# A gated mLSTM/Fourier mixer on one core: the output gate's sigmoid moves to the projection stage, the head gain into the weight rows

## The chip, the cores and the metric

The kernel runs on one core of one Trainium2 chip. The metric is the device time of the whole program in microseconds, as the median of several runs; lower is better. The engines are named as in the profile: PE is TensorE (PEld its weight loads), DVE is VectorE, ACT is ScalarE, POOL is GpSimd, SP is SyncE, which here only issues DMAs.

## The reference, cut to what matters

One layer is applied to 128 prompt tokens and 1024 latent tokens. The part that the change touches is the end of the mixer:

```python
p = (h @ w_in + b_in)
q, k, v, o = the four 512-wide blocks of p; gates = 16 columns; u = the last 512 columns
h_f, h_b = mlstm_chunkwise(forward), mlstm_chunkwise(backward)       # chunks of 128 tokens
hm = h_f + flip(h_b)
hm = hm * lax.rsqrt(mean(hm * hm, axis=-1) + EPS) * head_g[:, None, :]
hm = hm.reshape(B, T, 512) * jax.nn.sigmoid(o)
out = concatenate([hm, fu], axis=-1) @ w_out                         # fu: Fourier mixing of u
x = x + gate1 * out
```

After it come a second normalisation, a router with softmax, an expert-choice mixture of 16 experts, and a last normalisation. `head_g` has 4 heads of 128 values, `w_out` is 1024 x 1024, and the first 512 rows of `w_out` meet `hm`.

## The kernel before

The tokens are 9 tiles of 128 rows (tile 0 the prompt, tiles 1 to 8 the latents). Every engine runs its own program, written out by hand; engines meet through semaphores, and each stage ends in a barrier of all engines. The stages are `modulation`, `projection`, `recurrence` (the states at the chunk borders, and the Fourier part), `mixing`, `routing`, `experts` and `finish`. The order on each engine is the order of the code, so a waiting instruction holds back all that stands behind it on its engine.

`projection` takes one tile in each turn of `body`. PE forms five 512-wide blocks (`block_sum`, L428), DVE adds the bias and writes them into `pr` (L501), ACT keeps the turned q and k (L395) and, for the next tile, half of the turned input (`keep_h`, L368). SP stores blocks 1 to 3 of `pr` (k, v, o) into `kvo` once block 3 is kept (L330), then `qkT` (L332).

`mixing` is a software pipeline of 13 turns. In turn i, tile i gets its scores and its weights (`score`, `exponents`, `weigh`, `weighted`, `inter`, `intra`, `combine`, in two directions d = 0, 1); tile i-1 gets its output (`outputs`, and the turned `mixT`); tile i-2 is projected with `w_out` in two halves of 512 columns (`project`, L1112) and gets its residual (L1212, L1214); tile i-3 is normalised and turned (`turn_rows`, L1123; `h2T`, L1061, L1302) and, as tile i-4 one turn later, routed (L1131). On DVE the order of a turn is `exponents(0)`, `weighted(0)`, `outputs`, normalisation, `residual(0)`, `combine(0)`, `exponents(1)`, `weighted(1)`, `residual(1)`, `h2T`, `combine(1)`.

The output gate is made inside `mixing`, for tile i in turn i: ACT takes `og = exp(-o)` (`front`, L1017), DVE adds one (L1286) and takes the reciprocal (L1289), POOL multiplies by the row of `head_g`, broadcast to all partitions, into `gain` (L990), and one turn later DVE multiplies `hm` by `gain` (L1248).

`w_out` lies where the Fourier input `y` lay before, so its four loads of 1 MB can only be issued in `mixing` itself: SP issues them (L950) behind the first two tiles' loads (L935 to L938, L941), `head_g` and the router. In the trace a tile of `w_out` has the name `y`. Only PE waits for it, in turn 2, just ahead of the first `project`:

```python
if below(i, 3):
    pe.wait_ge(g.w_out_loaded, 16 * (DT // 2))
    pe.wait_ge(consts_loaded, 32)
project(i, par, 0)
```

Of the kernel before, what the change touches and what calls it, by code (L numbers as in the profile page):

```python
# [23 lines left out]
P = 128  # L24
D = 1024
DT = D // P
# [5 lines left out]
HEADS = 4  # L32
# [243 lines left out]
def projection(nc, g):  # L276

    ctx = ExitStack()
    with ctx:
# [32 lines left out]
        kvo_stored = [sem(f"kvo_stored{i}") for i in range(2)]  # L312
        qk_stored = sem("qk_stored")
        COLS = (0, WIDTH, 2 * WIDTH, 3 * WIDTH, OFF_F)

        with nc.Block() as block:
            @block.sync
            def _(sp):
# [9 lines left out]
                def store(i, par):  # L328
                    sp.wait_ge(block_kept, 5 * i + 4)
# [31 lines left out]
            def _(act):  # L361
# [23 lines left out]
                def body(i, par, half):  # L385
# [15 lines left out]
                tile_loop(act, g.act, body, {"squares_summed": 4, "hT_ready_act": 8, "qk_kept": 4, "y_kept": 4, "act_steps": 4})  # L401
# [452 lines left out]
def mixing(nc, g):  # L854
# [4 lines left out]
    with ctx:  # L859
# [13 lines left out]
        og, gain = sb("og", [P, WIDTH]), sb("gain", [P, WIDTH])  # L873
        head_g = sb("head_g_row", [P, WIDTH])
# [11 lines left out]
        def bank(name):  # L886
# [15 lines left out]
         hm_ready, hm_turned, mix_act, mix_pool, og_exped, og_ready, gain_ready, hms_ready, rh_ready, ss_steps) = (  # L902
# [4 lines left out]
                "aff_ready", "aff_turned", "aff_kept", "hm_ready", "hm_turned", "mix_act", "mix_pool", "og_exped",  # L907
                "og_ready", "gain_ready", "hms_ready", "rh_ready", "ss_steps"))
# [18 lines left out]
        with nc.Block() as block:  # L927
            @block.sync
            def _(sp):
                def load(i, par, fresh):  # L930
                    if not fresh:
                        sp.wait_ge(inter_summed, 2 * i - 2)
                        sp.wait_ge(intra_summed, 2 * i - 2)
                        sp.wait_ge(og_exped, i - 1)
                    sp.dma_start(qk[:, par].rearrange("p h n -> p (h n)"), g.qkT[bass.ts(i, P), :]).then_inc(qk_loaded[par], 16)  # L935
                    sp.dma_start(m_in[:, par], g.m_lanes[bass.ds(i, 1), :].to_broadcast([P, LANES * P])).then_inc(m_loaded[par], 16)
                    sp.dma_start(va[:, par, :, 0:HD], g.kvo[bass.ts(i, P), WIDTH:2 * WIDTH].rearrange("p (h v) -> p h v", v=HD)).then_inc(v_loaded[par], 16)
                    sp.dma_start(o_in[:, par], g.kvo[bass.ts(i, P), 2 * WIDTH:3 * WIDTH]).then_inc(o_loaded[par], 16)  # L938
# [6 lines left out]
                sp.dma_start(head_g[:], g.head_g.to_broadcast([P, WIDTH])).then_inc(consts_loaded, 16)  # L945
# [31 lines left out]
            def _(pool):  # L977
                pool.wait_ge(consts_loaded, 32)

                def turn(i, par, half):  # L980
# [875 lines left out]
```

## Time and profile before

| what | value |
|---|---|
| median of 3 runs | 2448.59 us (2448.11 to 2449.16) |
| the profiled execution | 2444.34 us, of which its span is 2442.5 us |
| granted TensorE clock, mean | 0.958 |
| PE busy | 2244.6 us (92%) |
| PEld busy | 1930.8 us (79%) |
| DVE busy | 486.6 us (20%) |
| ACT busy | 349.4 us (14%) |
| POOL busy | 154.3 us (6%) |

The stages lie at about 90 to 458 us (`projection`), 458 to 558 (`recurrence`), 558 to 800 (`mixing`) and 800 to the end (routing, experts, finish). Whole-span shares say little about one stage; the rows further down are read stage by stage.

### The profile page before, as it was taken

Reading aid. Unit: us, or ns where it says so; the run is one execution under the profiler, and the core shown is the slowest. Engines: PE = TensorE matmul, PEld = TensorE weight load, DVE = VectorE, ACT = ScalarE, POOL = GpSimd, SP = SyncE. Lnnn points to the kernel's source line nnn. Section 1 sums busy time; section 2 is a strip of 40 time slices with the busy share of each in tenths; the row PEclk is TensorE's granted clock in tenths of the full one; section 3 lists DMA queues with packets and bytes.
Section 4 is the critical chain, followed back from the end, with each engine's and each line's share of the span. In section 5 each row is a group of like instructions: output and inputs, shape, how many; then the busy total and the mean of one; then the engine's idle time right before and its main releaser. Section 6 shows DMA issues by size and latency. Waiting matters only on the chain. (4 is left out here: it accounts for less than half of the span.)

```text
span 2442.5 us, 37362 instructions
## 1 busy us (share of the span) xinstructions
PE 2244.6 (92%) x15311; PEld 1930.8 (79%) x15311; DVE 486.6 (20%) x1160; ACT 349.4 (14%) x1005; POOL 154.3 (6%) x184
## 2 busy tenths in 40 slices
PE   4799999875998299999999999999999999999993
PEld 0355545574564199999999999999999999999993
DVE  0111111537885600000000100000000000000002
ACT  0011111222332001111111111011111110111112
POOL 0000000011211000000000000000000000000002
PEclk7799999987999599999999999999999999999996
DMA  9610101215431776796886966968969769679674
GB/s 389 271 61 30 61 30 52 91 70 204 155 121 67 228 243 212 252 340 210 313 270 223 361 212 231 365 207 289 297 215 351 227 232 364 207 265 325 211 258 173
DMA packets 339783, 530.11 MB, mean 217 GB/s; under 512 B 10984, under 2 KB 282128, under 8 KB 335392
## 3 DMA queue, kind: packets, MB, share of 16 engines
q1 hardware_dynamic: 332144, 510.13, 60.0%
q0 software_dynamic: 7600, 19.47, 3.2%
q8 instruction: 23, 0.38, 0.1%
q14 instruction: 16, 0.13, 0.0%
HBM read 493.61 MB, written 35.95 MB: 217 GB/s over the span
## 5 line engine op out<-in xcount | busy, mean ns | idle before, releaser
L1522 PE MATMUL ps_ab<-xeT,ring 128*128 128x144 f32 x8192 | 1010.5, 287 | 2.3 <-DVE xeT L1570 2.3
L1522 PEld LDWEIGHTS ps_ab<-xeT,ring 128*128 128x128 f32 x8192 | 1007.2, 191 | 6.1 <-issue 6.1
L1537 PE MATMUL ps_yy<-hidT,ring 128*128 128x144 f32 x4096 | 505.6, 287 | 0.0
L1537 PEld LDWEIGHTS ps_yy<-hidT,ring 128*128 128x128 f32 x4096 | 502.6, 190 | 2.1
L428 PE MATMUL ps_p<-w_in_sb,hT 128*128 128x512 f32 x720 | 318.0, 596 | 4.5 <-DMA w_in_sb<-in_w_in 4.5
L1577 DVE TENSOR_TENSOR hidT<-silu,ps_ab 128x144 f32<-128x144 f32 x256 | 78.0, 305 | 929.2 <-ACT silu L1491 900.3
L428 PEld LDWEIGHTS ps_p<-w_in_sb,hT 128*128 128x128 f32 x720 | 135.0, 192 | 157.8 <-issue 157.4
L1491 ACT ACTIVATE silu<-ps_ab 128x144 f32<-128x144 f32 x256 | 74.3, 290 | 933.6 <-PE ps_ab L1522 933.6
L1112 PE MATMUL b_z<-y,mixT 128*128 128x512 f32 x288 | 128.0, 598 | 1.9 <-ACT aff L1048 1.7
L1585 DVE TENSOR_SCALAR ye<-ps_t,slot_gate 128x512 f32<-128x512 f32 x32 | 22.6, 747 | 486.3 <-PE ps_t L1547 486.3
L1468 POOL DMA_INDIRECT stream<-ye,slot_row x16 | 25.8, 1612 | 1362.5 <-DVE ye_p L1587 1362.5
L1496 ACT ACTIVATE yT<-ps_yy,mod 128x128 f32<-128x128 f32 x128 | 47.0, 367 | 420.8 <-PE ps_yy L1537 420.8
L1112 PEld LDWEIGHTS b_z<-y,mixT 128*128 128x128 f32 x288 | 53.3, 190 | 65.6 <-issue 62.8
L501 DVE TENSOR_TENSOR pr<-ps_p,b_in_row 128x512 f32<-128x512 f32 x45 | 31.1, 692 | 296.1 <-PE ps_p L428 296.1
L183 PE MATMUL ps_row<-y,vecT 128*2 128x512 f32 x128 | 26.1, 902 | 25.4 <-DMA y<-in_ada_w 25.4
L183 PEld LDWEIGHTS ps_row<-y,vecT 128*2 128x2 f32 x128 | 1.8, 84 | 47.3 <-DMA y<-in_ada_w 44.6
L693 PE MATMUL bk<-const,y 128*128 128x256 f32 x128 | 34.8, 398 | 0.0
L1497 ACT ACTIVATE yT_p<-ps_yy,mod 128x16 f32<-128x16 f32 x128 | 34.1, 266 | 0.0
L1482 ACT ACTIVATE xeT<-ps_t,mod 128x128 f32<-128x128 f32 x68 | 25.5, 456 | 58.5 <-PE ps_t L1504 58.5
L368 ACT ACTIVATE hT<-ps_x,mod 128x128 f32<-128x128 f32 x36 | 13.5, 456 | 124.7 <-PE ps_x L413 124.7
L1289 DVE RECIPROCAL og<-og 128x512 f32<-128x512 f32 x9 | 30.2, 3353 | 0.3
L1350 PE MATMUL ps_route<-prompt_slots,const 16*128 16x32 f32 x2 | 0.6, 406 | 31.9 <-DVE prompt_slots L1380 31.9
(256 smaller groups left out, 1167.1 us busy)
## 6 DMA issues: line engine op xcount, KB each, us to landing
ring<-in_exp_w SPq DMA_DIRECT2D x384, 1024.0 KB, 11.6
y<-in_ada_w SPq DMA_DIRECT2D x16, 1024.0 KB, 14.1
w_in_sb<-in_w_in SPq DMA_DIRECT2D x4, 2576.0 KB, 24.2
w_in_sb<-in_ada_w SPq DMA_DIRECT2D x8, 1024.0 KB, 14.7
kv<-kvo SPq DMA_DIRECT2D x15, 512.0 KB, 5.1
kvo<-pr SPq DMA_DIRECT2D x9, 768.0 KB, 3.3
qkT_dram<-qkT SPq DMA_DIRECT2D x9, 512.0 KB, 4.7
qk<-qkT_dram SPq DMA_DIRECT2D x9, 512.0 KB, 5.4
```

What stands on the lines that cost most here:

```text
L183: mm = nc.tensor.matmul(ps_row[grp][32 * j:32 * j + 2, :], vecT[:, k:16:DT], ada[n % RING][:, bass.ts(j, 512)], start=(k == 0), stop=(k == ...
L428: mm = nc.tensor.matmul(ps_p[(par + b) % 2][:], hT[:, par, k], g.w_in_sb[:, k, COLS[b]:COLS[b] + 512], start=(k == 0), stop=(k == DT - 1))
L501: g.dve.did(nc.vector.tensor_tensor(pr[:, par, b], ps_p[(par + b) % 2][:], g.b_in_row[:, COLS[b]:COLS[b] + 512], ALU.add), block_kept)
L693: mm = nc.tensor.matmul(bk[n % 2][:, 0:256], lhs, basis, start=(c == 0), stop=(c == 1))
L1112: mm = nc.tensor.matmul(b_z[h][:], mixT[:, par, k], g.w_out_sb[:, k, bass.ts(h, 512)], start=(k == 0), stop=(k == DT - 1))
L1289: did(nc.vector.reciprocal(og[:], og[:]), og_ready)
L1491: nc.scalar.activation(silu[:, f % 2], ps_ab[f % 2][:, 0:N], ACT.Silu).then_inc(silu_ready, 1)
L1496: nc.scalar.activation(yT[:, d], ps_yy[d % 2][:, 0:CAP_L], ACT.Copy, scale=g.mod[:, 1, 4, d:d + 1])
L1497: nc.scalar.activation(yT_p[:, d], ps_yy[d % 2][:, CAP_L:N], ACT.Copy, scale=g.mod[:, 0, 4, d:d + 1]).then_inc(yT_kept, 1)
L1522: mm = nc.tensor.matmul(ps_ab[f % 2][:, N * w:N * w + N], unit[:, k, bass.ts(c, P)], xeT[:, k], start=(k == 0), stop=(k == DT - 1))
L1537: mm = nc.tensor.matmul(ps_yy[d % 2][:, 0:N], unit[:, f % 2, bass.ts(d, P)], hT[:, f], start=(f == 0), stop=(f == FT - 1))
L1577: nc.vector.tensor_tensor(hT[:, f], silu[:, f % 2], ps_ab[f % 2][:, N:2 * N], ALU.mult).then_inc(h_kept, 1)
```

## The change

The sigmoid is taken by ACT in `projection`, in place, on block 3 of `pr` before it is stored, so that `o_in` in `mixing` holds the finished gate. `front`, the addition of one, the reciprocal, POOL's `gain`, and the tiles `og` and `gain` go. DVE multiplies `hm` by `o_in` directly. `head_g` is loaded as a column, one value for each partition and head, and ACT scales the first four row blocks of `w_out` with it (`scale_out`) at the end of its turn 0; PE's wait for `w_out` and the constants becomes a wait for these four instructions. In SP's `load`, the wait for `og_exped` goes, and the load of `o_in` waits for `hm_ready`, since `o_in` is now read by DVE.

```diff
                 def store(i, par):
-                    sp.wait_ge(block_kept, 5 * i + 4)
+                    sp.wait_ge(gate_o_ready, i + 1)
                     sp.dma_start(g.kvo[bass.ts(i, P), :], pr[:, par, 1:4].rearrange("p b n -> p (b n)")).then_inc(kvo_stored[par], 16)
...
                                                        ACT.Copy, scale=(1.0, K_SCALE)[j]), qk_kept)
+                    act.wait_ge(block_kept, 5 * i + 4)
+                    g.act.did(nc.scalar.activation(pr[:, par, 3], pr[:, par, 3], ACT.Sigmoid), gate_o_ready)
                     if not (isinstance(i, int) and i == TILES - 1):
                         keep_h(i + 1, 1 - par)
...
                         sp.wait_ge(intra_summed, 2 * i - 2)
-                        sp.wait_ge(og_exped, i - 1)
...
+                    if not fresh:
+                        sp.wait_ge(hm_ready, i - 1)
                     sp.dma_start(o_in[:, par], g.kvo[bass.ts(i, P), 2 * WIDTH:3 * WIDTH]).then_inc(o_loaded[par], 16)
...
-                sp.dma_start(head_g[:], g.head_g.to_broadcast([P, WIDTH])).then_inc(consts_loaded, 16)
+                with nc.allow_non_contiguous_dma("head gains, one per partition"):
+                    sp.dma_start(head_g[:], g.head_g.rearrange("a (h v) -> v (a h)", v=HD)).then_inc(consts_loaded, 16)
...
-                    if on(i, 0):
-
-                        pool.wait_ge(og_ready, i + 1)
-                        if not below(i, 1):
-                            pool.wait_ge(hm_ready, i)
-                        nc.gpsimd.tensor_tensor(gain[:], og[:], head_g[:], ALU.mult).then_inc(gain_ready, 1)
...
-                def front(i, par, half):
-                    act.wait_ge(o_loaded[par], 16 * (half + 1))
-                    if not below(i, 1):
-                        act.wait_ge(gain_ready, i)
-
-                    did(nc.scalar.activation(og[:], o_in[:, par], ACT.Exp, scale=-1.0), og_exped)
+                def scale_out():
+                    act.wait_ge(g.w_out_loaded, 16 * (DT // 2))
+                    act.wait_ge(consts_loaded, 32)
+                    for h in range(HEADS):
+                        did(nc.scalar.activation(g.w_out_sb[:, h], g.w_out_sb[:, h], ACT.Copy, scale=head_g[:, h:h + 1]), w_out_scaled)
...
                     if on(i, 0):
-                        front(i, par, half)
                         weigh(i, 0)
...
                         weigh(i, 1)
                         inter(i, 1)
+                    if below(i, 1):
+                        scale_out()
...
                         if below(i, 3):
-                            pe.wait_ge(g.w_out_loaded, 16 * (DT // 2))
-                            pe.wait_ge(consts_loaded, 32)
+                            pe.wait_ge(w_out_scaled, HEADS)
                         project(i, par, 0)
...
-                    dve.wait_ge(gain_ready, i)
-                    did(TT(hm[:], hm[:], gain[:].rearrange("p (h v) -> p h v", v=HD), ALU.mult))
+                    dve.wait_ge(o_loaded[1 - par], 16 * (half + par))
+                    did(TT(hm[:], hm[:], o_in[:, 1 - par].rearrange("p (h v) -> p h v", v=HD), ALU.mult))
...
                     if on(i, 0):
-                        dve.wait_ge(og_exped, i + 1)
-                        did(TS(og[:], og[:], 1.0, None, ALU.add))
                         weighted(i, 1)
-                        settle()
-                        did(nc.vector.reciprocal(og[:], og[:]), og_ready)
```

ACT, turns 0 and 1 of `mixing`, before (`wgt` is what `weigh` writes, `num` what `inter` writes, `b_i` the PSUM banks of `inter`):

```order
L1017 ACTIVATE og<-o_in 128x512 [waits o_loaded0]
L1021 ACTIVATE wgt<-wgt 128x512 [waits x_ready]
L1028 ACTIVATE num<-b_i,cols 128x129 [waits inter_summed]
L1028 ACTIVATE num<-b_i,cols 128x129 x3
L1021 ACTIVATE wgt<-wgt 128x512 [waits x_ready]
L1028 ACTIVATE num<-b_i,cols 128x129 [waits inter_summed]
L1028 ACTIVATE num<-b_i,cols 128x129 x3
L1017 ACTIVATE og<-o_in 128x512 [waits gain_ready,o_loaded1]
L1021 ACTIVATE wgt<-wgt 128x512 [waits x_ready]
L1028 ACTIVATE num<-b_i,cols 128x129 [waits hm_ready,inter_summed]
```

The same place on ACT in the changed kernel (`y` is `w_out`):

```order
L1016 ACTIVATE wgt<-wgt 128x512 [waits x_ready]
L1023 ACTIVATE num<-b_i,cols 128x129 [waits inter_summed]
L1023 ACTIVATE num<-b_i,cols 128x129 x3
L1016 ACTIVATE wgt<-wgt 128x512 [waits x_ready]
L1023 ACTIVATE num<-b_i,cols 128x129 [waits inter_summed]
L1023 ACTIVATE num<-b_i,cols 128x129 x3
L1012 ACTIVATE y<-y,head_g_col 128x1024 [waits consts_loaded,w_out_loaded]
L1012 ACTIVATE y<-y,head_g_col 128x1024 x3
L1016 ACTIVATE wgt<-wgt 128x512 [waits x_ready]
L1023 ACTIVATE num<-b_i,cols 128x129 [waits hm_ready,inter_summed]
```

The two instructions on `og` are gone, and four on `w_out`, the first with a wait for its loads, stand between turn 0 and the first weights of turn 1.

ACT, the first turn of `projection`, in the changed kernel (`pr` at L399 is the sigmoid):

```order
L396 ACTIVATE qkT<-ps_qk 128x512 [waits qk_turned] x2
L399 ACT_TABLE_LOAD
L399 ACTIVATE pr<-pr 128x512 [waits block_kept]
L369 ACTIVATE hT<-ps_x,mod 128x128 [waits x_turned]
L369 ACTIVATE hT<-ps_x,mod 128x128 x3
```

Before, the rows on `hT` stood directly behind those on `qkT`; the table load stands in the first turn alone.

## Rows read from the trace of the kernel before

**Rows 1.** Busy time by engine in stretches of the span (windows).

```profile
core 0: us, PE busy (x) PEld busy (x) DVE busy (x) ACT busy (x) POOL busy (x), PEclk, DMA share, GB/s
90.00:458.00 368.00, 360.84 (x1090) 183.54 (x1089) 55.53 (x118) 45.47 (x111) 4.39 (x8) 0.98 0.14 54
...
558.00:595.90 37.90, 18.45 (x100) 17.11 (x101) 25.16 (x48) 8.50 (x23) 4.62 (x5) 0.65 0.86 296
595.90:614.50 18.60, 18.60 (x78) 10.96 (x77) 16.19 (x29) 5.50 (x14) 3.19 (x3) 1.00 0.19 65
...
638.80:749.20 110.40, 108.59 (x495) 66.09 (x494) 97.61 (x201) 37.19 (x108) 20.38 (x30) 1.00 0.37 130
```

**Rows 2.** Instructions in order of time, turns 6 and 7 of mixing (start, us).

```profile
683.28 7.13 PE L1112 MATMUL b_z<-y,mixT 128*128 128x512 f32 x16
...
696.08 3.35 DVE L1289 RECIPROCAL og<-og 128x512 f32<-128x512 f32 x1
...
705.42 1.13 PE L1112 MATMUL b_z<-y,mixT 128*128 128x512 f32 x2
```

**Rows 3.** Costliest groups of instructions, by line: busy us, mean ns.

```profile
L1289 DVE RECIPROCAL og<-og 128x512 f32<-128x512 f32 x9 | 30.2, 3353 | 0.3
...
L256 ACT ACTIVATE squares<-xt 128x1024 bf16<-128x1024 f32 x7 | 7.4, 1057 | 37.9 <-DMA xt<-in_x_latent 37.9
...
L1017 ACT ACTIVATE og<-o_in 128x512 f32<-128x512 f32 x9 | 5.6, 619 | 14.8 <-DMA o_in<-kvo 9.0 <-POOL gain L990 5.8
...
L1286 DVE TENSOR_SCALAR og<-og 128x512 f32<-128x512 f32 x9 | 3.8, 421 | 0.0
```

**Rows 4.** Instructions in order of time, turns 0 to 2 of mixing.

```profile
571.72 1.12 ACT L1028 ACTIVATE num<-b_i,cols 128x129 f32<-128x129 f32 x4
...
578.66 0.63 ACT L1021 ACTIVATE wgt<-wgt 128x512 f32<-128x512 f32 x1 [0.60 <-DVE wgt L1195]
579.32 0.69 DVE L1201 TENSOR_TENSOR wgt<-wgt,b_s 128x512 f32<-128x512 f32 x1 [0.69 <-ACT wgt L1021]
...
586.72 1.14 ACT L1028 ACTIVATE num<-b_i,cols 128x129 f32<-128x129 f32 x4 [7.43 <-DVE hm L1251]
...
590.40 0.69 DVE L1201 TENSOR_TENSOR wgt<-wgt,b_s 128x512 f32<-128x512 f32 x1 [0.36 <-ACT wgt L1021]
...
595.92 7.03 PE L1112 MATMUL b_z<-y,mixT 128*128 128x512 f32 x16
```

**Rows 5.** The line that loads w_out: issues, and us to landing.

```profile
L950 SPq DMA_DIRECT2D y<-in_w_out x4: 449/671/1497, 568.6 to 571.5; - x4
...
DMA to landing us min/median/max: 9.5/12.0/14.3
```

**Rows 6.** Two stretches of 1 us while loads run (columns of rows 1).

```profile
570.00:571.00 1.00, 0.13 (x2) 0.00 (x0) 1.00 (x5) 0.00 (x0) 0.00 (x0) 1.00 1.25 263
...
576.00:577.00 1.00, 0.90 (x5) 0.60 (x3) 1.00 (x3) 0.00 (x0) 0.93 (x1) 0.50 1.02 410
```

**Rows 7.** Waits of PE from 595.5 to 770 us: total, times, longest.

```profile
PE b_z L1123 <- DVE x L1212: 3.4, 2, 2.6
PE b_z L1131 <- ACT h2T L1061: 2.5, 2, 1.2
```

**Rows 8.** Instructions in order of time, end of turn 3 of mixing.

```profile
629.68 3.35 DVE L1289 RECIPROCAL og<-og 128x512 f32<-128x512 f32 x1
...
633.73 1.06 PE L1123 MATMUL b_z<-const,xn 128*128 128x128 f32 x8 [2.59 <-DVE x L1212]
```

**Rows 9.** Instructions in order of time, last two tiles of projection.

```profile
407.80 1.50 ACT L368 ACTIVATE hT<-ps_x,mod 128x128 f32<-128x128 f32 x4 [7.23 <-PE ps_x L413]
...
416.17 7.03 PE L428 MATMUL ps_p<-w_in_sb,hT 128*128 128x512 f32 x16
...
447.54 0.43 SPq L332 DMA_DIRECT2D qkT_dram<-qkT  x1
...
457.84 0.66 ACT L383 ACTIVATE y<-ps_y 128x256 f32<-128x256 f32 x2 [1.22 <-PE ps_y L471]
```

More of the change, by code:

```diff
@@ L312, in projection @@
         kvo_stored = [sem(f"kvo_stored{i}") for i in range(2)]
+        gate_o_ready = sem("gate_o_ready")
         qk_stored = sem("qk_stored")
@@ L400, in _ @@
                 keep_h(0, 0)
-                tile_loop(act, g.act, body, {"squares_summed": 4, "hT_ready_act": 8, "qk_kept": 4, "y_kept": 4, "act_steps": 4})
+                tile_loop(act, g.act, body, {"gate_o_ready": 2, "squares_summed": 4, "hT_ready_act": 8, "qk_kept": 4, "y_kept": 4, "act_steps": 4})
                 keep_y(TILES - 1)
@@ L872, in mixing @@
         hms = sb("hms", [P, HEADS])
-        og, gain = sb("og", [P, WIDTH]), sb("gain", [P, WIDTH])
-        head_g = sb("head_g_row", [P, WIDTH])
+        head_g = sb("head_g_col", [P, HEADS])
         mixT = sb("mixT", [P, 2, DT, P])
@@ L901, in mixing @@
          logits_summed, logits_kept, logits_turned, negmax_ready, soft_exped, aff_ready, aff_turned, aff_kept,
-         hm_ready, hm_turned, mix_act, mix_pool, og_exped, og_ready, gain_ready, hms_ready, rh_ready, ss_steps) = (
+         hm_ready, hm_turned, mix_act, mix_pool, w_out_scaled, hms_ready, rh_ready, ss_steps) = (
             sem(n) for n in (
@@ L906, in mixing @@
                 "h2T_dve", "h2T_act", "logits_summed", "logits_kept", "logits_turned", "negmax_ready", "soft_exped",
-                "aff_ready", "aff_turned", "aff_kept", "hm_ready", "hm_turned", "mix_act", "mix_pool", "og_exped",
-                "og_ready", "gain_ready", "hms_ready", "rh_ready", "ss_steps"))
+                "aff_ready", "aff_turned", "aff_kept", "hm_ready", "hm_turned", "mix_act", "mix_pool", "w_out_scaled",
+                "hms_ready", "rh_ready", "ss_steps"))
         def group(t):
@@ L1070, in turn @@
                         square(i, par, 1)
-                turns(act, g.act, turn, {"og_exped": 2, "w_ready": 4, "inter_kept": 4, "act_steps": 18, "sq_summed": 4,
+                turns(act, g.act, turn, {"w_ready": 4, "inter_kept": 4, "act_steps": 18, "sq_summed": 4,
                                          "soft_exped": 2, "h2T_act": 2, "mix_act": 2})
@@ L1221, in combine, with outputs @@
                                ALU.add), comb_done if b else None)
-                def outputs(i):
+                def outputs(i, par, half):
                     settle()
@@ L1262, in turn @@
                     if on(i, 1):
-                        outputs(i)
+                        outputs(i, par, half)
                     if on(i, 4):
@@ L1307, in _ @@
                 turns(dve, g.dve, turn, {
-                    "dve_steps": 44, "x_ready": 4, "p_ready": 4, "og_ready": 2, "negmax_ready": 2, "out_kept": 4, "x2_ready": 4,
+                    "dve_steps": 42, "x_ready": 4, "p_ready": 4, "negmax_ready": 2, "out_kept": 4, "x2_ready": 4,
                     "comb_done": 4, "aff_ready": 2, "xn2_ready": 2, "aff_kept": 2, "h2T_dve": 2, "hms_ready": 2, "hm_ready": 2,
```

1 line of the change is left out of this document (removed).

## The prediction

> **What bounds the kernel now.** I read first the busy times by stretch, because the whole-span shares mix stages with different limits. In projection PE is busy for 360.84 of 368 us [rows 1]. Mixing falls into a ramp and a steady part. In the ramp, 558 to 595.9 us, no engine is full: PE 18.45 and DVE 25.16 of 37.9 us, ACT 8.50, at a mean granted clock of 0.65 of full speed [rows 1]. What sets its length is a chain of waits from engine to engine. From 595.9 us on, where the first `project` starts, PE is full: 18.60 of 18.60 us in turn 2, and 108.59 of 110.40 us from turn 4 to turn 8 [rows 1]. DVE has 97.61 of the same 110.40 us, so it is close behind PE, but behind.
>
> That PE is really at its limit there, and not only shown as busy, I take from the spacing: the 16 passes of one half of `project` take 7.13 us in turn 6, and the next turn's start comes 705.42 - 683.28 = 22.14 us later [rows 2]; the same 16 passes take 7.03 us in projection, where nothing else competes [rows 9]. The reciprocal of turn 6 runs from 696.08 us for 3.35 us [rows 2], beside these passes.
>
> Two things follow. Work taken off DVE in a steady turn pays only where PE waits for DVE. And a delay ahead of the first `project` pays in full, because PE is full from there on and can't catch up.
>
> **The steady turns.** The change takes off DVE, in each of 9 turns, the reciprocal (3.35 us) and the addition of one (0.42 us) [rows 3], 3.8 us together and 9 x 3.8 = 34 us in all. It takes 0.62 us each off ACT [rows 3] and the product with the gains off POOL. What PE waited for between 595.5 and 770 us stands in one table [rows 7]: 3.4 us in two waits of the turning of rows for a residual, and 2.5 us in two waits of the router for `h2T`. The longest, 2.59 us, ended at 633.73 us in turn 3 [rows 8]: PE was there at 633.73 - 2.59 = 631.14 us, while the reciprocal had held DVE from 629.68 to 633.03 us, and the residual that frees the PSUM bank stood behind it. Without the reciprocal, the residual starts at 629.7 us and is over at 630.4 us, ahead of PE. That wait goes: **-2.6 us**. The other wait of this kind is 3.4 - 2.6 = 0.8 us, and the router's two are about 1.25 us each. They are in the draining turns, where PE has no scores to do in between and waits for ACT's `h2T`, not for a reciprocal; I leave them as they are (between 0 and -1 us). So of 34 us of DVE work, 2.6 us are worth something. The cover of the rest is PE's own 22.1 us a turn.
>
> **The ramp.** Here ACT's new work stands. In turn 0 ACT finishes `inter` at 571.72 + 1.12 = 572.8 us [rows 4]. The next in its order is now `scale_out`, which waits for all four loads of `w_out`. The last was issued at 571.5 us; they land in order, and the longest takes 14.3 us [rows 5], so at 571.5 + 14.3 = 585.8 us. Before, only PE waited for them, at 595.9 us, so they were covered by 10 us. Now ACT stands still for some 13 us, and behind it stand the weights of turn 1 (L1021), for which DVE's `weighted` (L1201) waits, and behind that `outputs`, and ACT's and PE's second direction.
>
> When the loads land in the new kernel: the broadcast of `head_g`, 256 KB, is gone from ahead of them. At the 410 GB/s of a full stretch [rows 6] that is 0.64 us less. In its place are 512 pieces of 4 bytes. The nearest row is the stretch around the router's load, 1024 pieces of 64 bytes: 263 in place of 410 GB/s for one microsecond [rows 6], a loss of 0.36 us if all of it is the router's. Half of that is 0.2 us; if a 4-byte piece costs ten times as much, it is 2 us. I take 0.2 us, by the nearest row, so the loads land 0.4 us earlier, at 585.4 us (585.2 to 587.2).
>
> The scaling: four instructions of 128x1024. The only row of that size on ACT is L256 with 1057 ns [rows 3]. Four of 456 ns in a row took 1.50 us [rows 9], so each starts 0.35 us after the last and 0.11 us are overlapped. That makes about 0.95 us each, 3.8 us until the next instruction may start (3.6 to 4.2). ACT then comes to the weights of turn 1 at 585.4 + 3.8 = 589.2 us. From there to DVE's `weighted` it is 579.32 - 578.66 = 0.66 us [rows 4], so `weighted` starts at 589.9 us in place of 579.3 us: **+10.5 us**.
>
> Does the chain behind it get shorter? From `weighted` at 579.32 to the first `project` at 595.92 it is 16.6 us [rows 4]: DVE's `outputs` until ACT may go on at 586.72, the second direction until `weighted` at 590.40, then PE's `intra`, the turning of `hm`, scores and `inter`. The reciprocals of turns 0 and 1 stand behind the second `weighted` of their turn, not in this chain. The one of turn 0 did hold up the first exponents of turn 1, but now ACT is later than that by far. The addition of one lay beside ACT's exponentials. Gate times `hm` is one instruction of 128x512 as before. So the chain keeps its 16.6 us, and the first `project` starts at 606.4 us.
>
> A second unknown is PE's clock. In this ramp it is at a mean of 0.65, so PE's part changes between its two levels (1.2 and 2.4 GHz), and is at 1.00 once `project` runs [rows 1]. A longer idle time could leave `project` at the lower level for a while, or put a short piece of the chain at the higher one. The PE work between 590.4 and 595.9 us is at most 5.5 us, so half of that, 2.7 us, is what a full clock could give; I take the same for a loss, and zero for the sum.
>
> **Projection.** ACT gets nine sigmoids of 128x512, priced by the exponential of the same shape at 0.62 us [rows 3], and one table load. They stand between the turned k and `keep_h` of the next tile. `keep_h` began at 407.80 and ended at 409.3 us, while PE takes its result at 416.17 us [rows 9]: 6.9 us of cover for under 1 us of delay. The table load of the first turn falls into the time in which ACT waits for block 3. SP now stores k, v, o about 0.7 us later, and behind it stand `qkT` and the next x load. At the end of the stage the last `qkT` store is issued at 447.54 us, while ACT's last piece of y runs until 457.84 + 0.66 = 458.5 us [rows 9]; an issue that moves by 0.7 us has 11 us for its landing. Cost 0. If this cover were gone, the whole would cost 9 x 0.7 = 6 us.
>
> The Trainium skill has a rule that speaks against this step. "ScalarE: Activation LUTs", section "What ACT_TABLE_LOAD costs", puts a switch of the set at about 2.66 us with its drain, and its rules ask to group functions by set. By that rule the sum would be 2.7 us higher. The rows show the cover instead.
>
> SP's new wait for `hm_ready` holds back only what waits for later results of the same turn anyway, and `o_in` is used a turn later: 0.
>
> **Sum.** +10.5 - 2.6 + 0 = +7.9 us. Against the profiled execution's own 2444.34 us that gives 2452.2 us. That execution is 4.25 us under the median of the runs, 2448.59 us; the forecast for the median is 2448.6 + 7.9 = **2456.5 us**.
>
> **The rivals.**
>
> *DVE paces the steady turns (faster).* If PE is stretched by waits that the rows don't name, a turn is worth the 3.8 us that DVE loses. Seven turns (2 to 8) give -26, with the ramp +10.5 - 26 = -16 us: 2433 us. It decides once DVE needs longer than PE for its turn. Against it: 97.61 against 108.59 us busy [rows 1] and the even spacing. For it: DVE is 88% busy, with short waits between.
>
> The Trainium skill, "Perfetto Trace Analysis", section "Identifying the Most-Contended Engine", says that matmul busy time is a poor measure and that weight-load busy time is the better one. PEld has 66.09 of 110.40 us [rows 1], 60%, under DVE's 88%; by that page DVE would be the one to relieve.
>
> *The ramp is paced by DVE and gives the stall back (no change).* Then turns 1, 2 and 3 are each shorter by 3.8 us: 10.5 - 11.4 = -0.9 us, 2447.7 us. For it: DVE is the busiest engine of the ramp. Against it: turn 2 is 18.60 of 18.60 us of PE, and no reciprocal lies in the chain of turn 1.
>
> *The stall is longer (slower still).* The 4-byte pieces cost 2 us and the clock 2.7 us more: 7.9 + 1.8 + 2.7 = +12.4 us, 2461 us.
>
> *The gain is not there, or the stall is smaller, because the scale waits only for loads that had landed.* The order of ACT and the landing times exclude it; it has no chance of its own.
>
> **How the numbers follow.** The forecast has 0.66, the longer stall 0.15, the ramp that gives back 0.13, the faster case 0.06. The forecast's own range is 2453 to 2460 us. The bounds of the loads, the scaling and the clock make 2452.5 to 2461.5 us, which leaves out the two cases below it and is the range that I give. A measurement of this kernel can tell about 0.2%, 4.9 us, from no change. Faster: 0.06. Within it: 0.13 and a little of the forecast's lower end, 0.16. Slower: 0.78.
>
> **What would show it.** In the profile after: an idle time of ACT of about 12 us before L1012, released by the load of `w_out`, ending near 585 us; four instructions of about 1 us; the first `project` near 606 us; steady turns of still 22.1 us, with DVE near 16 of 22; no wait of PE before the turning of rows in turn 3; projection as long as before. I am wrong if the turns get shorter than 22 us, if the first `project` starts before 602 us, or if projection grows.

## The result, and the profile of the changed kernel

| what | before | changed | difference |
|---|---|---|---|
| median | 2448.04 us (20 runs, 2441.95 to 2450.31) | 2451.78 us (20 runs, 2449.16 to 2456.61) | +3.7 us |
| ratio of times, 95% interval | | 1.002 (1.0014 to 1.0027) | +3.4 to +6.6 us |
| profiled execution | 2444.34 us, span 2442.5 | 2451.03 us, span 2449.0 | +6.7 us |

The changed kernel is slower by 0.2%. The forecast was +7.9 us. The sign was right and the place too, but the amount is above the interval. The medians differ by 3.7 us and the means of the same runs (2447.25 and 2452.26 us) by 5.0 us. The predicted 2456.5 us is 4.7 us above the measured median, which lies 0.7 us below the lower end of the given range. In the table of the experiments, the medians of i and k and of the kernel before beside i, j and k include one or two disturbed executions of over 3000 us (without them they are 2441.19, 2448.53 and 2448.74 us); the ratios leave these out.

The page of the changed kernel, its part 1 (engine, busy us, share, instructions):

```profile
PE 2249.7 (92%) x15311; PEld 1933.7 (79%) x15311; DVE 448.8 (18%) x1142; ACT 356.3 (15%) x1010; POOL 143.3 (6%) x175
```

DVE lost 486.6 - 448.8 = 37.8 us of work and the kernel still got slower. The windows of the changed kernel answer to [rows 1], with the columns of those:

```profile
90.00:458.00 368.00, 360.55 (x1091) 183.26 (x1091) 56.09 (x118) 52.07 (x122) 4.41 (x8) 0.98 0.14 54
558.00:607.90 49.90, 21.49 (x100) 20.14 (x101) 18.15 (x47) 12.27 (x26) 2.56 (x3) 0.54 0.66 224
607.90:626.50 18.60, 18.60 (x78) 10.95 (x78) 12.30 (x29) 4.97 (x14) 1.39 (x2) 1.00 0.24 83
648.00:758.20 110.20, 108.80 (x498) 66.23 (x497) 77.60 (x193) 35.61 (x104) 14.56 (x27) 1.00 0.36 126
```

Projection is as long as before, with 6.6 us more of ACT in it. The ramp grew from 37.9 to 49.9 us. Over five steady turns DVE fell from 97.61 to 77.60 us, and PE has 108.80 us where it had 108.59. What fills the ramp is in the instructions of the changed kernel in order of time, ACT, DVE and PE, which answer to [rows 4] (L1012 scales `w_out`, whose name in the trace is `y`; in brackets the idle time ahead and what ended it):

```profile
572.43 1.13 ACT L1023 ACTIVATE num<-b_i,cols 128x129 f32<-128x129 f32 x4
585.61 4.26 ACT L1012 ACTIVATE y<-y,head_g_col 128x1024 f32<-128x1024 f32 x4 [12.05 <-DMA y<-in_w_out]
589.78 0.61 ACT L1016 ACTIVATE wgt<-wgt 128x512 f32<-128x512 f32 x1
...
590.43 0.69 DVE L1196 TENSOR_TENSOR wgt<-wgt,b_s 128x512 f32<-128x512 f32 x1 [13.13 <-ACT wgt L1016]
...
591.17 2.09 PE L1098 MATMUL b_n<-va,wgt 128*128 128x129 f32 x8 [13.47 <-DVE wgt L1196]
...
601.82 0.69 DVE L1196 TENSOR_TENSOR wgt<-wgt,b_s 128x512 f32<-128x512 f32 x1 [0.69 <-ACT wgt L1016]
...
607.94 7.03 PE L1108 MATMUL b_z<-y,mixT 128*128 128x512 f32 x16
```

ACT stands still for 12.05 us until the load of `w_out` ends the wait, and 13.13 us of DVE and 13.47 us of PE hang on it. The steady turns and the wait in turn 3 of the changed kernel, PE in order of time, beside [rows 2] and [rows 8]:

```profile
642.11 1.06 PE L1098 MATMUL b_n<-va,wgt 128*128 128x129 f32 x8
643.00 1.04 PE L1119 MATMUL b_z<-const,xn 128*128 128x128 f32 x8
...
691.98 7.13 PE L1108 MATMUL b_z<-y,mixT 128*128 128x512 f32 x16
...
713.98 1.55 PE L1108 MATMUL b_z<-y,mixT 128*128 128x512 f32 x3
```

L1119 follows with no idle time, where it had waited 2.59 us. A steady turn takes 713.98 - 691.98 = 22.00 us, after 22.14.

### The profile page after: what moved, and what is told of

The parts are those of the page before. It is cut to its first block and busy times, and to the rows that moved or that the text cites. A ratio compares the mean times of both kernels' runs of the same rounds, so it can differ in the third digit from the quotient of the medians.

```text
span 2449.0 us, 37315 instructions
## 1 busy us (share of the span) xinstructions
PE 2249.7 (92%) x15311; PEld 1933.7 (79%) x15311; DVE 448.8 (18%) x1142; ACT 356.3 (15%) x1010; POOL 143.3 (6%) x175
## 5 line engine op out<-in xcount | busy, mean ns | idle before, releaser
L183 PE MATMUL ps_row<-y,vecT 128*2 128x512 f32 x128 | 27.4, 946 | 22.3 <-DMA y<-in_ada_w 22.3
L1098 PE MATMUL b_n<-va,wgt 128*128 128x129 f32 x144 | 23.2, 312 | 17.0 <-DVE wgt L1196 17.0
L1098 PEld LDWEIGHTS b_n<-va,wgt 128*128 128x128 f32 x144 | 21.0, 222 | 20.5 <-DVE wgt L1196 18.1
```

The source lines that it names most:

```text
L183: mm = nc.tensor.matmul(ps_row[grp][32 * j:32 * j + 2, :], vecT[:, k:16:DT], ada[n % RING][:, bass.ts(j, 512)], start=(k == 0), stop=(k == ...
L1098: mm = nc.tensor.matmul(b_n[h // 2][:, VW * (h % 2):VW * (h % 2) + VW], wgt[:, d, h], va[:, par, h], start=True, stop=True)
```

## The experiments

All starts below are read from one profiled execution of each kernel. "Start" is the first load that SP issues in mixing, "first project" is where the first 16 passes with `w_out` begin, "last half" where those of the last tile's second half begin, "end of mixing" the first issue of the experts' weights by SP, which follows the stage's barrier. The start itself moves between profiles of one and the same kernel: from 558.10 to 559.04 us in the three of the kernel before, 558.81 and 559.23 us in the two of the changed kernel. A difference of under 1 us between two absolute times is therefore not told apart from none, and where it matters the times are counted from the start.

| kernel | start | first project | turn 3 | turn 4 | last half | end of mixing | median | before, same chip | ratio, 95% |
|---|---|---|---|---|---|---|---|---|---|
| before | 558.58 | 595.92 | 614.56 | 638.80 | 777.69 | 800.05 | 2448.04 | | |
| changed | 559.23 | 607.94 | 626.59 | 648.04 | 786.07 | 808.42 | 2451.78 | 2448.04 | 1.0014 to 1.0027 |
| a: stall alone | 559.10 | 609.21 | 627.85 | 650.89 | 789.78 | 813.59 | 2456.27 | 2445.66 | 1.0034 to 1.0062 |
| b: no scaling | 558.59 | 592.31 | 610.95 | 632.41 | 770.39 | 792.74 | 2435.07 | 2445.66 | 0.9944 to 0.9971 |
| c: gain in projection | 558.50 | 592.20 | 610.84 | 632.29 | 770.29 | 792.63 | 2437.37 | 2445.66 | 0.9954 to 0.9978 |
| d: changed again | 558.81 | 606.95 | 625.59 | 647.04 | 785.05 | 807.40 | 2451.00 | 2445.66 | 1.0009 to 1.0027 |
| e: before again | 558.10 | 596.56 | 615.20 | 639.39 | 778.31 | 800.66 | 2447.12 | 2447.31 | 0.9992 to 1.0010 |
| f: scaled twice | 558.38 | 611.51 | 630.15 | 651.61 | 789.61 | 813.88 | 2457.68 | 2447.31 | 1.0030 to 1.0057 |
| g: scaled in mid turn 1 | 559.40 | 600.54 | 619.19 | 640.64 | 778.63 | 802.89 | 2445.52 | 2447.31 | 0.9983 to 1.0001 |
| h: scaled at end of turn 1 | 559.01 | 592.84 | 611.56 | 633.01 | 771.01 | 793.36 | 2439.18 | 2447.31 | 0.9960 to 0.9984 |
| i: no reciprocal in before | 557.75 | 594.58 | 613.22 | 634.68 | 773.25 | 797.51 | 2441.21 | 2449.06 | 0.9964 to 0.9984 |
| j: no sigmoid | 559.32 | 607.42 | 626.06 | 647.51 | 785.90 | 811.57 | 2452.95 | 2449.06 | 1.0011 to 1.0032 |
| k: before, third time | 559.04 | 597.10 | 615.74 | 641.80 | 780.27 | 804.53 | 2448.59 | 2449.06 | 0.9990 to 1.0008 |

**a. The stall alone, put into the kernel before.**

```diff
+                def scale_out():
+                    act.wait_ge(g.w_out_loaded, 16 * (DT // 2))
+                    act.wait_ge(consts_loaded, 32)
+                    for h in range(HEADS):
+                        did(nc.scalar.activation(g.w_out_sb[:, h], g.w_out_sb[:, h], ACT.Copy, scale=1.0), g.w_in_loaded)
...
                         inter(i, 1)
+                    if below(i, 1):
+                        scale_out()
...
-                            pe.wait_ge(g.w_out_loaded, 16 * (DT // 2))
-                            pe.wait_ge(consts_loaded, 32)
+                            pe.wait_ge(g.w_in_loaded, 16 * 4 + HEADS)
```

> The kernel before, with one thing of the change alone: at the end of its turn 0 in mixing ACT waits for w_out and copies its first four row blocks in place, times one; PE waits for these copies. Sigmoid, reciprocal and gain stay as before. Theory (the stall of ACT delays the first project, and nothing gives it back): ACT idle about 12 us before the copies, the first project near 607.9 us in place of 595.9 us, and with the reciprocal still there no wait is won in turn 3, so mixing ends about 12 us later than before and the time is +9 to +12 us. Rival (the ramp gives it back, since DVE paced it): first project at 600 us or earlier, time within 3 us of before.

ACT of this kernel in order of time:

```profile
586.45 3.89 ACT L1023 ACTIVATE y<-y 128x1024 f32<-128x1024 f32 x4 [13.10 <-DMA y<-in_w_out]
590.25 0.61 ACT L1017 ACTIVATE og<-o_in 128x512 f32<-128x512 f32 x1
590.77 0.61 ACT L1027 ACTIVATE wgt<-wgt 128x512 f32<-128x512 f32 x1
```

The loads end 586.45 - 559.10 = 27.4 us behind the start, where the changed kernel and d, f, g and j have 26.3 to 26.6 us. This fits the 256 KB of `head_g` that are ahead of them, though no run changes this load alone. `og` stands in the way for 0.5 us more. First `project` moves by 609.21 - 595.92 = +13.3 us. Turn 3 gives back 1.2 us of that: it takes 650.89 - 627.85 = 23.04 us, in the kernel before 638.80 - 614.56 = 24.24 us, since PE's wait for the residual is 1.4 us here and 2.6 us there. The steady part gives nothing back: from turn 4 to the last half it is 789.78 - 650.89 = 138.89 us, in the kernel before 777.69 - 638.80 = 138.89 us. The expected +9 to +12 us holds: the median is +10.6 us, the ratio is worth 11.7 us. So a delay ahead of the first `project` pays almost in full: here 1.2 of 13.3 us went into a later wait that became shorter.

**b. The changed kernel without the scaling.** `head_g` is left out of the computation; the rest stands.

```diff
-                    if below(i, 1):
-                        scale_out()
...
-                            pe.wait_ge(w_out_scaled, HEADS)
+                            pe.wait_ge(g.w_out_loaded, 16 * (DT // 2))
+                            pe.wait_ge(consts_loaded, 32)
```

> The changed kernel without the scaling of w_out: head_g is not multiplied in at all, PE waits for the loads of w_out as in the kernel before. Theory of the stall: the first project comes at 595 to 597 us in place of 607.9 us, the mixing stage ends about 12 us earlier than in the changed kernel and 3 to 4 us earlier than before: time -3 to -4 us against before. Rival (DVE paces the steady turns): then the turns are shorter than 22 us and the time is over 15 us under before.

The expectation missed on both counts: it had the first `project` at 595 to 597 us and the time 3 to 4 us under before. First `project` is at 592.31 us, 3.6 us ahead of the kernel before, mixing ends 800.05 - 792.74 = 7.3 us earlier, and the median is 10.6 us lower (the spans of the two profiles differ by 9.4 us, 2.1 of them behind mixing).

Against the changed kernel it is 607.94 - 592.31 = 15.6 us, of which 0.6 us are the later start of the stage. So the stall costs some 15 us, not 12: it also covers 3.6 us that the change had won in the ramp. Where they come from is to be seen on ACT and DVE. The kernel before, in order of time, turn 0 to turn 1:

```profile
566.15 0.63 ACT L1017 ACTIVATE og<-o_in 128x512 f32<-128x512 f32 x1 [8.99 <-DMA o_in<-kvo]
566.68 0.61 ACT L1021 ACTIVATE wgt<-wgt 128x512 f32<-128x512 f32 x1
...
571.84 0.69 DVE L1201 TENSOR_TENSOR wgt<-wgt,b_s 128x512 f32<-128x512 f32 x1 [0.36 <-ACT wgt L1021]
572.57 3.35 DVE L1289 RECIPROCAL og<-og 128x512 f32<-128x512 f32 x1
...
575.84 0.69 DVE L1220 TENSOR_TENSOR num<-num,b_n 128x258 f32<-128x258 f32 x2
576.07 1.27 POOL L990 TENSOR_TENSOR gain<-og,head_g_row 128x512 f32<-128x512 f32 x1 [28.31 <-DVE og L1289]
576.44 2.18 DVE L1195 SCALAR_TENSOR_TENSOR wgt<-m_in,cols,const 128x128 f32<-128x128 f32 x4
```

And the same place in kernel c, which has no stall either:

```profile
565.58 0.63 ACT L1017 ACTIVATE wgt<-wgt 128x512 f32<-128x512 f32 x1 [8.51 <-DVE wgt L1190]
...
570.76 0.69 DVE L1196 TENSOR_TENSOR wgt<-wgt,b_s 128x512 f32<-128x512 f32 x1 [0.69 <-ACT wgt L1017]
...
572.77 0.76 DVE L1215 TENSOR_TENSOR num<-num,b_n 128x258 f32<-128x258 f32 x2 [1.32 <-PE b_n L1097]
573.45 1.13 DVE L1190 SCALAR_TENSOR_TENSOR wgt<-m_in,cols,const 128x128 f32<-128x128 f32 x4
575.27 0.69 DVE L1196 TENSOR_TENSOR wgt<-wgt,b_s 128x512 f32<-128x512 f32 x1 [0.69 <-ACT wgt L1017]
```

`weighted` of turn 1 comes at 575.27 in place of 579.32 us, 4.05 us earlier, and this has three parts. Some 1.1 us were there before the reciprocal: in the kernel before, ACT's `og` of turn 0 waits for the load of `o_in` and holds the first weights until 566.68 us, and the second `weighted` of turn 0 starts at 571.84 in place of 570.76 us. The reciprocal then holds back the `combine`, which starts 4.00 us behind this `weighted` in place of 2.01: 2.0 us. From there to `weighted` of turn 1 it is 3.48 in place of 2.50 us, since the exponents take 2.18 us in place of 1.13 while POOL's product runs: 1.0 us. Of the 4.05 us, 3.6 to 3.7 reach the first `project`.

**c. The gain multiplied in projection.** Everything is computed. POOL multiplies block 3 of `pr` by the row of `head_g` behind the sigmoid, SP stores behind that, and `mixing` has no scaling and no load of `head_g`; PE waits for the loads of `w_out` as in b.

```diff
                 def store(i, par):
-                    sp.wait_ge(gate_o_ready, i + 1)
+                    sp.wait_ge(gate_o_scaled, i + 1)
...
+                def scale(i, par):
+                    pool.wait_ge(gate_o_ready, i + 1)
+                    nc.gpsimd.tensor_tensor(pr[:, par, 3], pr[:, par, 3], head_g[:], ALU.mult).then_inc(gate_o_scaled, 1)
...
                         invert_rms(nc, g, pool, i, par)
+                        scale(i - 1, 1 - par)
...
-                    if below(i, 1):
-                        scale_out()
```

> The full computation without touching w_out: the broadcast row of head_g is loaded in projection, and POOL multiplies the sigmoid by it there, ahead of the store of k, v, o. Theory: POOL's nine products of 1.3 us lie beside PE's 41 us a tile and cost nothing; mixing runs as without the scaling, so -3 to -5 us against before, -8 to -12 us against the changed kernel. Rival: the store comes 2 us later at each tile and lengthens projection by up to 9 x 1.3 us: +6 to +9 us against before.

2437.37 us, 0.34% (8.3 us) under the kernel before and 13.6 us under the changed kernel on the same chip, both more than the 3 to 5 and 8 to 12 us that were expected. Projection is not longer; the windows of c, columns as above:

```profile
90.00:458.00 368.00, 360.63 (x1089) 183.12 (x1089) 55.67 (x118) 51.69 (x122) 15.82 (x17) 0.98 0.14 55
```

POOL has 11.4 us more there, beside 360.63 us of PE. This is the version to keep: it does the whole of the change, with the gain in a place where PE does not wait for it.

**f, g, h. The scaling twice, or at another place.** In f four more instructions with scale 1.0 stand ahead of the four. In g and h the call is moved:

```diff
                     if on(i, 0):
                         weigh(i, 0)
+                    if isinstance(i, int) and i == 1:   # g: here
+                        scale_out()
...
                         weigh(i, 1)
                         inter(i, 1)
-                    if below(i, 1):
-                        scale_out()
+                    if isinstance(i, int) and i == 1:   # h: here
+                        scale_out()
```

> The changed kernel with the four instructions on w_out doubled: four copies times one ahead of the four with the gain. Theory (what ACT does between its turn 0 and the weights of turn 1 goes one to one into the end of mixing): the scaling takes 8.4 us in place of 4.26, the first project comes at 611 to 612 us, time +4.2 us against the changed kernel, some +10 against before. Rival (part of the delay is made good in later turns): under +2 us against the changed kernel.

> The changed kernel with the scaling moved by one place on ACT, behind the first weights of turn 1 (ahead of the num copies that wait for hm). DVE can then go on with the outputs of tile 0 while the loads land. Theory: weighted(1,0) at 575 us as in the run without scaling; ACT waits until 585.5 us, is free at 589.8 us in place of 583.0 us, so the first project comes about 6.8 us later than 592.2 us, near 599 us, and the time is within 2 us of before. Rival (it is the length of ACT's wait that counts, not its place): the first project stays near 607 us.

> The changed kernel with the scaling at the end of turn 1, behind the num copies of the second direction and ahead of the copy into mixT. The loads have landed by then, so ACT does not wait, and it is on ACT from 587.7 to 591.9 us. PE can start the first project once mixT is copied, at 592.5 us in place of 592.2 us. Theory: time -6 to -8 us against before, within 1 us of the run with the gain in projection. Rival (4.2 us of ACT work in the ramp cost their own time wherever they stand): first project near 596.4 us, time -3 to -4 us against before.

ACT of kernel f in order of time:

```profile
584.79 3.89 ACT L1012 ACTIVATE y<-y 128x1024 f32<-128x1024 f32 x4 [13.14 <-DMA y<-in_w_out]
588.71 4.26 ACT L1015 ACTIVATE y<-y,head_g_col 128x1024 f32<-128x1024 f32 x4
592.88 0.61 ACT L1019 ACTIVATE wgt<-wgt 128x512 f32<-128x512 f32 x1
```

Four instructions more are 3.9 us more on ACT. First `project` moves by 3.6 us against the changed kernel and by 4.6 us against d; counted from the start of the stage it is 4.4 and 5.0 us. The medians are 6 us apart, over the expected 4.2; 1.9 us of this are a longer stretch behind the last half (24.27 in place of 22.35 us), which comes and goes in kernels of both kinds. The time that ACT is held passes through to PE.

ACT of kernel h in order of time:

```profile
586.98 1.13 ACT L1023 ACTIVATE num<-b_i,cols 128x129 f32<-128x129 f32 x4
587.99 4.27 ACT L1012 ACTIVATE y<-y,head_g_col 128x1024 f32<-128x1024 f32 x4
592.14 0.60 ACT L1064 ACTIVATE mixT<-b_m 128x512 f32<-128x512 f32 x1
```

Here the loads have landed when ACT comes to them: no wait. The same four instructions cost 592.84 - 592.31 = 0.5 us of first `project`, counted from the start 0.1 us, against some 15 us one turn earlier. The rival, 4.2 us wherever they stand, had 596.4 us. The time is the expected 6 to 8 us under before (6.9 by the ratio), 1.4 us more than c by the ratios. In g the wait for the landing is still there (until 586.03 us), but `outputs` of tile 0 runs on DVE meanwhile. It costs 600.54 - 592.31 = 8.2 us (7.4 from the start; 6.8 were expected, and the rival had the first `project` near 607 us), about what the change wins, and the ratio to the kernel before is not told apart from 1.

**i. The kernel before without the reciprocal.** The gate is exp(-o) alone; addition and reciprocal are left out, POOL's product and ACT's `og` stay, with POOL now waiting for `og`.

```diff
-                        pool.wait_ge(og_ready, i + 1)
+                        pool.wait_ge(og_exped, i + 1)
...
-                        dve.wait_ge(og_exped, i + 1)
-                        did(TS(og[:], og[:], 1.0, None, ALU.add))
                         weighted(i, 1)
-                        settle()
-                        did(nc.vector.reciprocal(og[:], og[:]), og_ready)
```

> The kernel before with one thing left out: no addition of one and no reciprocal (the gate is exp(-o) itself). Sigmoid, gains and all waits of ACT and POOL stay in mixing. It measures what 9 x 3.8 us off DVE are worth without the stall. The first runs say: weighted of turn 1 starts about 4 us sooner, since the reciprocal of turn 0 stands ahead of its exponents, and the turns lose 3.6 us together. So the first project near 592.3 us, mixing ends 6 to 7.3 us earlier than before, time -6 to -8 us against before. My sum had only -2.6 us for it. Rival (the gain came from ACT's and POOL's removed work as well): under -4 us.

Turn 3 goes from 638.80 - 614.56 = 24.24 to 634.68 - 613.22 = 21.46 us, as in the changed kernel (21.45). This shows the reciprocal as the cause of the wait in turn 3. The whole is 0.26% faster: 34 us less work on DVE bring 6 to 8 us (the ratio is worth 6.4 us, the undisturbed medians are 7.6 us apart), as expected.

The first `project` is a miss. It was expected near 592.3 us and comes at 594.58 us, only 1.3 us ahead of the kernel before, 0.8 of which are the earlier start. The trace has the reciprocal's 3.0 us as in b: 2.01 us from `weighted` to `combine` and 2.50 us on to the next `weighted`. But ACT's `og` of turn 0 is still ahead of the first weights, as the rival had it in part (1.0 us), and PE was at its lower level where the first profile of before was not: the first `intra` of turn 0 took 2.09 us, in that profile 1.16, and from 590 to 594.5 us the granted clock is 0.50, where that profile has 0.69 in its last 3.9 us before `project`.

**j. The changed kernel without the sigmoid.** `o` itself is stored as the gate.

```diff
-                    act.wait_ge(block_kept, 5 * i + 4)
-                    g.act.did(nc.scalar.activation(pr[:, par, 3], pr[:, par, 3], ACT.Sigmoid), gate_o_ready)
```

> The changed kernel without the sigmoid in projection (the raw o is stored and used as the gate, no table load, the store waits for block 3 as before). It prices the sigmoid's place. Theory (covered by PE in projection): projection ends at the same 458 us, the first project near 607 us, time within 1.5 us of the changed kernel. Rival: nine sigmoids and one table load lie on the path, -3 to -9 us against the changed kernel.

First `project` at 607.42 us, between the changed kernel (607.94) and d (606.95), and a median that isn't lower: against the kernel before, j is at 1.0022 and the changed kernel at 1.0020 and 1.0018. The nine sigmoids cost nothing that these runs can tell, and the rival's 3 to 9 us are excluded.

**d, e, k. The two kernels again.** No edit.

> The changed kernel as it is, on the same chip as the others, for a second profile. Mixing ends 8.4 us later than before again. If the part of it that the time does not show is the moment at which the granted clock rises, then the stretch from the end of mixing to the end of the span differs between the profiles of one kernel by about as much (1 to 4 us) as between kernels.

> The kernel before, unchanged, for a second profile and a second median. The profiled execution shown with it lay 4.3 us under the median of its runs. If the ramp of mixing in that profile had by luck of the granted clock been short, then in this profile the first project comes later than 595.9 us, by 1 to 4 us, and the changed kernel's loss against it is smaller than the 8.4 us of the first pair. Rival: the first project is at 595.9 us again, and the difference lies behind mixing or ahead of it.

> The kernel before once more, for a third profile: where the granted clock is in the ramp of mixing, and what the first project and the end of mixing are. If the clock there differs from execution to execution, the first project moves by 1 to 3 us between the profiles of one and the same kernel, while the steady turns stay at 22.1 us.

The changed kernel gives twice the same span (2449.0 us). In d mixing ends 7.4 us later than in the first profile of before, where 8.4 were expected, and from there to the end of the span it is 1641.6 us, in the first profile of the changed kernel 1640.6 us. In e the first `project` is 0.6 us later than in the first profile, under the 1 to 4 us expected. From the start it is 1.1 us, most of it the first `intra` of turn 0, which took 2.09 us (as in k) in place of 1.16. Of the kernel before there are now three profiles, with spans of 2442.5, 2442.6 and 2446.5 us. The third is the one whose execution, 2448.35 us, agrees with the median; the other two lie 3.7 and 2.7 us under theirs. k differs from the first profile by +1.2 us at first `project` (0.5 of them the start of the stage), +1.8 us in turn 3, -0.4 us from turn 4 to the last half, and +1.9 us behind it: together the 4.5 us by which mixing ends later. The windows of k in turn 3 show the second of these (PEclk is the last column but two):

```profile
634.00:636.00 2.00, 0.91 (x9) 0.94 (x10) 1.97 (x3) 0.00 (x0) 1.27 (x1) 1.00 0.00 0
636.00:638.00 2.00, 2.00 (x13) 2.00 (x12) 2.00 (x7) 1.80 (x5) 0.00 (x0) 0.58 0.44 176
638.00:640.00 2.00, 2.00 (x12) 1.88 (x11) 1.29 (x5) 1.89 (x5) 0.74 (x3) 0.56 0.99 311
```

The same stretch of the kernel before, first profile:

```profile
636.00:638.00 2.00, 2.00 (x20) 1.77 (x19) 1.92 (x7) 1.89 (x5) 0.24 (x1) 1.00 0.85 256
638.00:640.00 2.00, 2.00 (x11) 1.20 (x10) 1.20 (x4) 0.69 (x2) 1.31 (x3) 1.00 1.00 281
```

In k the granted clock falls to 0.58 and 0.56 behind PE's wait of 2.77 us; in the first profile, behind a wait of 2.59 us, it stays at 1.00, and in e, where turn 3 takes 24.19 us, it does too.

## Why the prediction was right, and where it was off

| step | forecast | profile of the changed kernel |
|---|---|---|
| landing of `w_out` | 585.4 us | 585.61 us |
| scaling until ACT goes on | 3.8 us | 4.17 us |
| `weighted` of turn 1 | +10.5 us | +11.1 us (590.43) |
| chain to first `project` | 16.6 us | 17.5 us |
| first `project` | 606.4 us | 607.94 us, +12.0 (+11.4 from the start) |
| PE's wait in turn 3 | -2.6 us | -2.8 us |
| turns 4 to the last half | 0 (to -1) | 138.03 after 138.89 us, -0.9 |
| projection | 0 | 0 (first issue of mixing 559.23 after 558.58) |
| end of mixing | +7.9 us | +8.4 us |
| behind mixing | 0 | -1.9 us |
| span | +7.9 us | +6.5 us |

**The end of mixing** is met within 0.5 us, in part by luck: the ramp came out 1.5 us longer than forecast, 0.65 us of this only by the later start of the stage, and turn 3 and the turns behind it gave back 1.1 us more.

**The stall** was right in its kind, its place and, within 1.5 us, its size. Kernel a has it alone, f makes it longer, h takes away the wait and leaves the work. The scaling was priced from a single row of L256 and came out 0.4 us low.

**The chain behind it** did not keep its 16.6 us. In the changed kernel PE had stood still for 13.5 us, and the granted clock was 0.50 from 580 to 604 us and 0.61 from 604 to 608, where the kernel before had 0.70 in its last 4 us before `project`. The first `project` came 6.12 us behind the second `weighted` (before 5.52). These 0.6 us are the clock's (the scores between them took 1.91 in place of 1.31 us), a term that the prediction named with up to 2.7 us on either side and put at zero. The other 0.3 us lie between the two `weighted` (11.39 us, before 11.08), and are not the clock's. The last step of `outputs` on DVE became longer, beside a copy of POOL that had stood elsewhere before. The changed kernel, then the kernel before:

```profile
596.89 0.60 POOL L1000 COPY mixT<-fuT 128x512 f32<-128x512 f32 x1
597.04 1.01 DVE L1246 TENSOR_TENSOR hm<-hm,hms 128x512 f32<-128x512 f32 x1 [0.98 <-POOL hms L986]
```

```profile
585.93 0.69 DVE L1251 TENSOR_TENSOR hm<-hm,hms 128x512 f32<-128x512 f32 x1 [0.98 <-POOL hms L984]
```

**The step that failed in its reasoning, though not in the sum,** is the sentence that the reciprocals stand in no chain of the ramp that counts. For the changed kernel it was true, since ACT came later. For the kernel before it was wrong as a statement of what the change could win: b and c start `project` 3.6 to 3.7 us earlier, and the reciprocal of turn 0 holds `weighted` of turn 1 back by 3.0 us with what follows from it. Another 1 us was ACT's `og` of turn 0, which the sum had at nothing: it waited for a load, and the first weights stood behind it. The stall took all this away unseen, so it cost some 15 us and with the gain elsewhere, as in c, the change is worth some 8 us. The rival in which the ramp gives the stall back counted a reciprocal for each of turns 1, 2 and 3; what is in the ramp is one, that of turn 0, and the stall lies over it.

**DVE does not pace the steady turns.** DVE's share of a turn fell from 88% to 70%, and a turn went from 22.14 to 22.00 us. The Trainium skill, "Perfetto Trace Analysis", section "Identifying the Most-Contended Engine", would have PE judged by its weight loads, beside a share of peak work that nothing here gives; PEld was busy for 60% of these turns in both kernels, and PE was the limit nonetheless. The trace doesn't agree with the weight-load part of that rule here.

**Projection** had the cover that the rows showed: j is not faster. "ScalarE: Activation LUTs", section "What ACT_TABLE_LOAD costs", in the Trainium skill, had spoken against the step; the one table load is there, with 1.28 us, but in front of a wait of 5.70 us. ACT in the first turn of projection, changed kernel:

```profile
122.84 1.28 ACT L399 ACT_TABLE_LOAD   x1
129.82 0.63 ACT L399 ACTIVATE pr<-pr 128x512 f32<-128x512 f32 x1 [5.70 <-DVE pr L504]
```

**The term that made the number too high** is, by what the profiles show, the last one: "the forecast for the median is 2448.6 + 7.9". It adds a difference that was worked out in one execution to the median of others. The profiled execution was 4.25 us under the median, and I took this for an offset common to both kernels. The changed kernel's profile has none (2451.03 against 2451.78 us). By the third profile of the kernel before, the change costs 10.8 us at first `project`, gives back 4.6 in turn 3, 0.4 up to the last half and 1.9 behind it, so mixing ends 808.42 - 804.53 = 3.9 us later. That this is so near the 3.7 us of the medians is luck in part: the 1.9 us are no property of the change, the span is only 2.5 us longer than that of k, and the means are 5.0 us apart. The times themselves say it more plainly. The kernel before has six of its twenty times from 2441.95 to 2445.18 us, with a mean of 2444.1, and fourteen from 2447.03 to 2450.31 us, with a mean of 2448.6; the mean of the changed kernel is 2452.3 us. Against the lower six the change costs 8.2 us, against the others 3.6. The forecast took its difference from an execution of the lower kind and set it on a median of the upper. The wait in turn 3 that the change removes costs 2.6 us, and in k 1.8 us more, with the clock lower behind it.

**What stays open.** That the fall of the clock in turn 3 is part of what sets the upper group of the kernel before apart rests on one profile against two. The 1.9 us behind the last half are the clock too, but they come and go in both families (22.35 us in before, e, b, c, d, h and the changed kernel, 23.8 us in a, 24.3 us in f, g, i and k, 25.7 us in j), and no run tells why. The 1.9 us given back behind mixing depend on the pair of profiles: from the end of mixing to the end of the span it is 1642.5, 1641.9 and 1642.0 us in before, 1640.6 and 1641.6 us in the changed kernel. They are in part the experts' start: the first profile of before has a clock of 0.50 for some 5.5 us there, the changed kernel for some 3 us.

## What to carry to other kernels

Before a step is put into an engine's program, look at what stands behind it there: four instructions of 1 us cost some 15 us where they waited for a load, and 0.5 us one turn later, where it had landed. Work that is taken off an engine pays only where another one waits for it; a table of waits showed that of 34 us on DVE some 3 us count, and the ramp, where no engine is full, has to be followed instruction by instruction for the rest. That holds for short instructions too, if they wait for a load: ACT's `og` of 0.6 us was worth 1 us there. A difference worked out from one execution should not be set on a median that lies beside it without asking which stretches of that execution the clock made short.

## What the runs showed of the hardware

**The same program meets another clock from execution to execution.** The three profiles of the kernel before end mixing at 800.05, 800.66 and 804.53 us. The work is the same; 0.5 us of the 4.5 are the start of the stage. In the tail of mixing, behind the last half, the windows of kernel g and of the kernel before (first profile) read:

```profile
785.60:802.90 17.30, 9.16 (x54) 5.85 (x52) 7.25 (x22) 4.46 (x14) 0.94 (x3) 0.77 0.15 61
```

```profile
784.70:800.00 15.30, 7.22 (x54) 5.11 (x52) 7.26 (x22) 4.46 (x14) 0.94 (x3) 1.00 0.17 70
```

The same 54 instructions keep PE busy for 9.16 us at a mean granted clock of 0.77 and for 7.22 us at 1.00, with waits for other engines in between in both. 0.50 and 1.00 are the two levels of the clock, 1.2 and 2.4 GHz.

**DVE is held up beside POOL.** In the kernel before, the first of the four exponent instructions beside POOL's product takes 1.04 us, three times its usual 0.35, and the second, which runs into POOL's copy behind the product, 0.69 us (name, ns min/median/max, kernel before, the line of the exponents in 574 to 600 us):

```profile
L1195 DVE SCALAR_TENSOR_TENSOR wgt<-m_in,cols,const x12: 337/348/1044, 576.4 to 596.8; 128x128 f32<-128x128 f32 x12
```

In kernel i, where POOL's product falls elsewhere, the longest of 72 takes 0.35 us. The Trainium skill, "SBUF — State Buffer", section "SBUF: two separate sides", says that a DVE instruction with two inputs in SBUF and a GpSimd instruction that reads SBUF exclude each other for the length of one. The trace agrees for DVE: the first instruction is 0.7 us longer beside a product of 1.27 us, all four together 1.05 us, and the step of `outputs` shown above is 0.3 us longer beside POOL's copy. It may also be why DVE lost 20.0 us in five steady turns, where the removed instructions are 5 x 3.77 = 18.9 us.
